# Up and gate projections of a feed-forward block: high and low input side by side in one product of 512 columns

## The reference, cut to what matters

```
D_FF = -(-8 * D_MODEL // (3 * 256)) * 256          # 2816 = 22 x 128

def swiglu(h, w_gate, w_up, w_down):
    return (jax.nn.silu(h @ w_gate) * (h @ w_up)) @ w_down

    h = rmsnorm(x, ffn_pre_g[l])
    x = x + rmsnorm(swiglu(h, w_gate[l], w_up[l], w_down[l]), ffn_post_g[l])
```

## Time and profile before

| | us |
|---|---|
| profiled execution, its own time | 1495.81 |
| its span, first to last instruction | 1494.0 |
| around the span | 1.8 |
| median of three runs | 1497.78 |
| steps f and down products (TensorE) | about 231 to 409 |
| expert layer | about 600 to 1490 |

### The profile page before, as it was taken

One profiled execution on the slowest core, in us unless ns is written; L12 is line 12 of the kernel. 1 busy time (PEld: TensorE's weight loads), 2 busy tenths in 40 slices (PEclk: granted clock), 3 DMA queues, 4 the chain that ended last, 5 costly groups with the idle time before them and its releaser, 6 DMA issues.

```text
span 1494.0 us, 20251 instructions
## 1 busy us (share of the span) xinstructions
PE 1156.1 (77%) x8876; PEld 779.3 (52%) x8876; DVE 443.3 (30%) x879; ACT 379.1 (25%) x836; POOL 69.3 (5%) x83
## 2 busy tenths in 40 slices
PE   9999999999998997897556567566665665675677
PEld 8998989999976875442223223223222232232234
DVE  5555777545678854010000000000000000000002
ACT  5655566444555644110000000000000000000002
POOL 0000020000033411000000000000000000000000
PEclk9999999999998998898778787877777787877888
DMA  8435546555553388999999999999999999999996
GB/s 316 166 138 202 197 170 233 204 198 198 198 179 119 104 341 362 376 434 441 426 437 429 431 434 433 436 431 430 436 427 440 425 438 429 434 433 432 428 421 275
DMA packets 29164, 503.37 MB, mean 337 GB/s; under 512 B 4114, under 2 KB 4754, under 8 KB 8084
## 3 DMA queue, kind: packets, MB, share of 16 engines
q1 hardware_dynamic: 25200, 493.43, 79.4%
q10 hardware_dynamic: 3876, 8.65, 1.7%
HBM read 501.02 MB, written 1.05 MB: 336 GB/s over the span
## 4 chain that ended last, share of the span: by engine, by line
issue 63%; PE 31%; DVE 3%; ACT 2%; POOL 1%; DMA 0%; POOLq 0%; DVEq 0%; ACTq 0%
PE PB L99 30%; PE PB L102 1%; DVE SPL L108 1%; ACT SPH L105 1%; POOL SPL L108 0%; DVE XN L116 0%; DVE AQK L108 0%; DMA RAW<-in_wst_dram 0%; POOL SM L136 0%; POOL SP L112 0%; ACT XN L105 0%; DVE SM L128 0%; ACT SP L105 0%; DVE XQL L108 0%; DVE RT L108 0%
## 5 line engine op out<-in xcount | busy, mean ns | idle before, releaser
L99 PE MATMUL PB<-RING,XS 128*32 128x512 f32 x2048 | 297.6, 731 | 173.8 <-DMA RING<-in_wgu_dram 170.0
L99 PEld LDWEIGHTS PB<-RING,XS 128*32 128x32 f32 x2048 | 69.3, 128 | 347.3 <-DMA RING<-in_wgu_dram 185.2
L99 PE MATMUL PB<-RING,HHT 128*32 128x256 f32 x2048 | 152.3, 456 | 108.9 <-DMA RING<-in_wdn_dram 106.6
L108 DVE TENSOR_TENSOR SPL<-RAW,SPH 128x512 fp32r<-128x512 f32 x316 | 209.0, 719 | 42.3 <-ACT SPH L105 40.1
L99 PE MATMUL PB<-XTH,SPL 128*128 128x256 f32 x704 | 201.7, 287 | 0.0
L99 PE MATMUL PB<-XTH,SPH 128*128 128x256 f32 x704 | 199.2, 283 | 0.0
L99 PE MATMUL PB<-XTL,SPH 128*128 128x256 f32 x704 | 199.1, 283 | 0.0
L105 ACT ACTIVATE SPH<-RAW 128x512 fp32r<-128x512 f32 x340 | 186.8, 621 | 12.1 <-DMA RAW<-in_wst_dram 5.3
L99 PEld LDWEIGHTS PB<-RING,HHT 128*32 128x32 f32 x2048 | 72.2, 130 | 173.7 <-DMA RING<-in_wdn_dram 110.6
L105 ACT ACTIVATE SG<-PB 128x512 f32<-128x512 f32 (+1 forms) x21 | 11.9, 566 | 510.0 <-PE PB L99 508.7
L99 PEld LDWEIGHTS PB<-XTL,SPH 128*128 128x128 f32 x704 | 135.0, 192 | 0.5
(11 more groups left out here) (315 smaller groups left out, 1353.7 us busy)
## 6 DMA issues: line engine op xcount, KB each, us to landing
RAW<-in_wst_dram SPq DMA_DIRECT2D x84, 1024.0 KB, 4.8
RING<-in_wgu_dram SPq DMA_DIRECT2D x13, 2048.0 KB, 40.5
RING<-in_wgu_dram SPq DMA_DIRECT2D x14, 1024.0 KB, 9.0
RING<-in_wdn_dram SPq DMA_DIRECT2D x6, 2048.0 KB, 13.5
RING<-in_wgu_dram SPq DMA_DIRECT2D x2, 4096.0 KB, 19.5
RING<-in_wdn_dram SPq DMA_DIRECT2D x2, 4096.0 KB, 17.9
RING<-in_wdn_dram SPq DMA_DIRECT2D x3, 1024.0 KB, 42.8
RAW<-in_wst_dram SPq DMA_DIRECT2D x4, 256.0 KB, 5.6
```

Of the source, the lines that this page charges most:

```text
L99: return pe.do(lambda e: e.matmul(out_, lhsT, rhs, start=start, stop=stop), after)
L108: return on.do(lambda e: e.tensor_tensor(out_, a, b, op), after)
```

## The change

XTH and XTL are now the two halves of one tile XT, at the same addresses as before, so that the high and low input tile of one k can be read as one moving operand of 2 x 256 columns (two runs of 256, 8 KB apart). In the 22 steps f a k-step is then two products: high weights by both inputs, 512 columns, into the whole bank, and low weights by the high input, 256 columns, added to the bank's first half. When the eight k-steps are through, the second half of the bank still has to be added to the first: ACT copies it to a tile FL, and DVE adds the first half to that. This is so for the gate product and for the up product. Silu then reads FL instead of PSUM, and the product of both reads two SBUF tiles. All other users of XTH and XTL work as before, under the name XT.

```diff
-    XTH = place("XTH", [P, KD, T], F32R, at(15))
-    XTL = place("XTL", [P, KD, T], F32R, at(23))
+    XT = place("XT", [P, 2, KD, T], F32R, at(15))
+    XTH, XTL = XT[:, 0, :, :], XT[:, 1, :, :]
...
+    FL = [place(f"FL{i}", [P, T], F32, at(195 + i)) for i in range(4)]
...
-        s = FT[f % 2]
-        a = act(s[:, :], PB[b0][:, 0:T], ACT.Silu, w0, hid.get(("m", f - 2)), w_out_done)
-        held[b0] = [a]
-        m = tt(FT[2 + f % 2][:, :], s[:, :], PB[b1][:, 0:T], ALU.mult, w1, a, hid.get(("lo", f - 2)))
-        held[b1] = [m]
+        s, g, v = FT[f % 2], FL[f % 2], FL[2 + f % 2]
+        a = act(g[:, :], PB[b0][:, T:512], ACT.Copy, w0, hid.get(("silu", f - 2)), w_out_done)
+        d = tt(g[:, :], g[:, :], PB[b0][:, 0:T], ALU.add, a)
+        held[b0] = [d]
+        hid["silu", f] = a = act(s[:, :], g[:, :], ACT.Silu, d, hid.get(("m", f - 2)), w_out_done)
+        b = act(v[:, :], PB[b1][:, T:512], ACT.Copy, w1, hid.get(("m", f - 2)), w_out_done)
+        d = tt(v[:, :], v[:, :], PB[b1][:, 0:T], ALU.add, b)
+        held[b1] = [d]
+        m = tt(FT[2 + f % 2][:, :], s[:, :], v[:, :], ALU.mult, d, a, hid.get(("lo", f - 2)))
         hid["m", f] = m
         h = act(HTH[:, f % 8, :], FT[2 + f % 2][:, :], ACT.Copy, m, hfree.get(f - 8))
         hid["lo", f] = tt(HTL[:, f % 8, :], FT[2 + f % 2][:, :], HTH[:, f % 8, :].bitcast(F32), ALU.subtract, h, hfree.get(f - 8))
 
     def wblock_ffn(uu, s, b):
-        return wblock(uu, s, b, XTH, XTL, xt)
+        hi, lo, got = unit(uu)
+        hv = hi[:, :].rearrange("p (k c) -> p k c", k=KD)
+        lv = lo[:, :].rearrange("p (k c) -> p k c", k=KD)
+        both = PB[b][:, :].rearrange("p (w t) -> p w t", w=2)
+        for k in range(KD):
+            after = [got[k // 2], *xt] + (held[b] if k == 0 else [])
+            mm(both, hv[:, k, s * P:(s + 1) * P], XT[:, :, k, :], k == 0, False, *after)
+            t = mm(PB[b][:, 0:T], lv[:, k, s * P:(s + 1) * P], XTH[:, k, :], False, k == KD - 1)
+        if s == 1:
+            unit_free[uu] = t
+        bg(2)
+        return t
```

## The result

Nine runs of the changed kernel took 1492.26 to 1495.33 us, median 1493.63; nine of the kernel before had the median 1497.78. The ratio is 0.9979 with a 95% interval of 0.9970 to 0.9988: 3.1 us faster, between 1.8 and 4.5. The profiled execution took 1493.10 us, span 1491.4.

The account below looks back on a forecast made before the run. PE alone was taken to set the changed layer's length, the tail following it. 0 (ACT, DVE) - 4.6 (PE) = -4.6 us, from the median 1497.78 to 1493.2 us, range 1490.5 to 1498.0.

Parts of the forecast that it names:

- each product carries a fixed 120.0 - 107.3 = 12.7 ns whatever its width: Gate and up products on PE: one fixed part less per k-step, 352 in all, saves 4.6 us.
- So nothing is added: Weight loads of the wide and narrow products stay hidden beside the product ahead, at no added time.
- The other rule: The Trainium skill's N/2.4 + 2.5 ns between products, by which the saving would be 0.9 us instead of 4.6.
- ACT and DVE cost nothing: Two more operations per step on each engine, 17 us busy time each, stay hidden beside PE: cost 0.
- With five pieces ACT was to fall behind: Steps with five split pieces: ACT loses 0.57 us a step, 2.3 us by f = 20, unseen by PE.
- HTL of f = 21: Last hidden tile before its down product: ready 5.0 us after the downs' start, leaving 1.8 us of cover.
- The addresses: Wide product's moving operand in two runs of 256 columns, 8 KB apart: bounded between free and 56 us more.
- the free end: The change of run inside the wide product's moving operand costs nothing, so it takes 227.3 ns.
- The tail moves with PE: Everything behind the changed layer, expert stage included, shifts one for one with PE, so the end comes 4.6 us earlier.
- rival of a gain given back: Behind the layer, a DMA wait or another clock pattern eats 2 to 4 us: about 1496.5 us; chance 0.09.

Follow-up runs that it names:

- e2_group: The changed kernel with the eight wide products of a block first, then its eight narrow ones: 1493.04 us, ratio 0.9977.
- e9_group16: The changed kernel with sixteen wide products (gate, then up) first in each step, then sixteen narrow ones: 1493.46 us, ratio 0.9979.
- e7_cols128: The kernel before with each k-step's third product split into two of 128 columns, each with its own weight load: 1535.3 us beside 1493.66.
- e4_chain: The kernel before, its products unchanged, with an added ACT copy and DVE maximum for each bank: 1496.87 us beside 1495.86, ratio 1.0004.
- e1_contig: The changed kernel with XT laid out k by k, so the wide product's 512 input columns are contiguous: 1493.71 us, ratio 0.9982.
- e6_plus: The changed kernel with four more, overwritten products of 256 columns at the head of each of the 44 blocks: 1516.42 us, ratio 1.0129.
- e2_again: The changed kernel with eight wide, then eight narrow products per block, measured a second time with more rounds: 1492.30 us, ratio 0.9969.

## Why the prediction was right, and where it was not

**Right in direction and time.** 1493.2 was forecast, 1493.63 measured, faster by 0.21% by the ratio. But the size of the mechanism was overestimated about twofold, and that the time came out within 0.5 us is luck: by the medians the gain was 4.15 us, by the ratio 3.1 (1.8 to 4.5), by the layer 2.36.

**The term that was mis-sized** is "each product carries a fixed 120.0 - 107.3 = 12.7 ns whatever its width", hence 352 x 12.7 = 4.5 us. Measured are 352 x 6.7 = 2.36. The fixed part was read from two streams, one all narrow and one all wide, and then used for a mixed one; in the mixed order a pair of a wide and a narrow product costs 6.6 ns more than the two do in streams of their own, and the order alone makes that difference (e2_group, e9_group16).

**Why a wide product behind narrow ones is late stays open.** The sentence on the weight loads, "So nothing is added", took today's 120.0 ns as proof that a load is hidden behind 256 columns. e7_cols128 shows that this is close: loads start no less than 111 ns apart, so a load beside a narrow product has under 10 ns to spare. It would be easy to make that the cause. But in the grouped kernel the second to fifth wide products are late too (235.0, 228.2, 232.0 and 230.4 ns for 226.7), and their loads start with a wide product ahead of them that gives twice the room. Lack of room beside the narrow product doesn't explain these, and no run here tells what does.

**The other rule.** The 2.5 ns that the prediction weighed against its own would have given 0.9 us; 2.4 came. Neither number fits this order, and the grouped orders (3.9 and 4.3 us in the layer) come up to the prediction's. The section of the Trainium skill from which it is, "Back-to-back issue gap" in "TensorE: Matmul & The Clock Gate", calls its formula the gap of an isolated product, which at small widths leaves out the weight load. Every product here has a load of its own, and 120.0 and 226.7 ns stand where the formula has 109.2 and 215.8.

**ACT and DVE cost nothing**: right, and nearly to the digit. e4_chain has the layer of before to 0.01 us. With five pieces ACT was to fall behind by 0.57 us a step against 5.56; it takes 6.08 us instead of 6.13. HTL of f = 21 was expected 5.0 us after the downs' start. The timelines of PE and DVE have it:

```profile
399.80 0.40 PE L99 MATMUL PB<-SPH,HTL 128*128 128x512 f32 x1
...
406.61 0.39 PE L99 MATMUL PB<-SPH,HTL 128*128 128x512 f32 x1
```

```profile
403.89 0.43 DVE L108 TENSOR_TENSOR HTL<-FT,HTH 128x256 fp32r<-128x256 f32 x1 [0.48 <-ACT HTH L105]
```

403.89 + 0.43 is 4.5 us after the start and 2.3 before its product, where 1.8 were forecast. That fits the smaller lag: ACT falls behind by 0.43 us a step instead of 0.57, since PE's step is 5.65 us instead of 5.56 and ACT's 6.08 instead of 6.13.

**The addresses**: the free end was right (e1_contig). The Trainium skill's sentence in "Advanced Engine Details and Errata", section "PSUM Cachelines", on access patterns that aren't contiguous does not reach a moving operand in two runs of 256: 178.35 us with the two runs and with one. No run here writes PSUM, of which that section speaks, in pieces.

**The tail moves with PE**: right as to the sense, since 21.1 us more in the layer were 22.7 us more at the end, give or take some 2; one for one to the microsecond is not shown. From the layer's end to the expert stage it was 594.23 - 407.49 = 186.74 us, before 595.65 - 408.77 = 186.88. The expert stage took 891.19 where it had 892.40, in three more traces with this order 891.43 to 892.05, in e4_chain, which has the products of before, 892.10: too close to call it the change's doing.

In the grouped kernels part of the gain is given back behind the layer, in all three traces. From the end of the layer's last product to the expert stage the four traces of the changed order have 186.53 to 186.84 us, the three grouped ones 187.45 to 187.79; the expert stage takes 891.19 to 892.05 in the four, 892.60 to 893.20 in the three. Together that is about as much as grouping saves in the layer (1.5 to 2.0 us), and the prediction's rival of a gain given back is not refuted for them. TensorE's clock differs as that rival had it: the granted clock is 0.83 in 470 to 490 us in the four traces and 0.74 to 0.76 in the three, 0.74 and 0.66 in 585 to 605. But the kernel before has 0.74 and 0.66 too and takes 186.92, so it is not shown that the clock is the cause.

Why the ratios of all four kernels with this layer (0.9977 to 0.9982) say about 3 us where the layer saves 2.4 stays open; each interval includes 2.4.

## What to carry to other kernels

Merging two products into a wider one saves less than the fixed part that uniform streams show: before counting on it, read the stream with the same neighbours, because the cost of a product from a uniform stream doesn't hold in a mixed one. Where a stream has wide and narrow products, put those of one width together, as far as open banks and the readers allow; that took another 1.5 us off the layer here, beyond the 2.4 of the change, though the time doesn't show it. A product of half the width is no bargain where each has its own weight load. And a chain of copies and additions on other engines may double in length without cost, if one lays out a whole period with the durations of rows and finds its last wait inside the cover.

## What was not expected of the hardware

- A product of 128 columns with its own load of 128 x 128 costs nearly what one of 256 does: four pairs of load and product took 462.5 ns, three 360.0.
- The first few wide products behind narrow ones are late, later ones not. In the kernel before too, the first down products start 0.23 and 0.24 us apart (253.76, then the rows below), while 48 take 227.3 ns each and the steady ones 226.7.

```profile
253.99 0.40 PE L99 MATMUL PB<-SPL,HTH 128*128 128x512 f32 x1
254.23 0.39 PE L99 MATMUL PB<-SPH,HTH 128*128 128x512 f32 x1
```

- The layer's start differed by up to 2.2 us between executions, 227.70 to 229.94, though nothing ahead of it was changed. The first 18 products of the chain of waits go with it: 5.33 to 5.66 us in before, e4_chain, e6_plus and e9_group16, whose layers start at 227.70 to 228.17, and 7.07 to 7.11 in the others (e1_contig's chain starts differently, with the same four products), whose layers start at 229.11 to 229.94. Four products of 512 columns among them make the difference, before and after:

```profile
4.33 2.26 PE L99 MATMUL PB<-GROW,WARM 1*128 1x512 f32 x4
4.34 3.78 PE L99 MATMUL PB<-GROW,WARM 1*128 1x512 f32 x4
```

  From the second on they follow one another after 0.43 us before and 0.85 after, a factor of two, which is that of TensorE's two clock levels. The clock records of the kernel before have it at the full level from 4.93 us, at the half level from 8.35 and full again from 15.17; those of the changed kernel begin with the full level at 15.65. (The stretch tables count time ahead of the first record as 1.00.) Over all eleven traces the layer starts the later, the later this last rise comes: 14.71 to 15.38 us in the four, 15.65 to 17.50 in the seven. e9_group16 and e2_again have the same program up to the layer and fall on either side, so it is the execution and not the edit that decides; what brings the clock up early, no experiment asked. The profiled executions of before and after differ by 1.1 us in this, which hides half of what the layer saves until one looks at the layer alone.
